# The last quarter of a down projection: six of its eight tiles as Strassen block products

## The chip, the cores and the metric

The kernel runs on one core of a Trainium2 chip, as one launch. The time is device microseconds (us) of that core, from runs of the whole kernel. Smaller is better. The core's engines work beside each other, each through its own instruction stream in order, and wait for one another on semaphores: PE (TensorE, matrix products), DVE (VectorE), ACT (ScalarE), POOL (GpSimd) and SP (which here only issues DMA).

## The reference

Two blocks of a network on 512 positions of 1024 channels, in float32. The change lies in the last step of the second block, a feed-forward layer, and touches the final norm behind it:

```python
h = rms_norm(x, norm2_g[l])
u = causal_dwconv(jnp.einsum('bsd,df->bsf', h, w_up[l]), ffn_conv_w[l])
gate, up = jnp.split(u, 2, axis=-1)
x = x + jnp.einsum('bsf,fd->bsd', jax.nn.gelu(gate) * up, w_down[l])
```

`w_up` is 1024 x 6144 and `w_down` 3072 x 1024. After it the result is normed once more (`final_g`).

## The kernel before, in words

**Layout.** Channels lie on the 128 partitions, positions along the row: `x1[:, j, :]` is tile j (0 to 7) of the result's 1024 channels, 128 x 512. A product in float32 is made of three products of rounded operands (`mm3`, lines 1160 to 1164): high part by high part, low by high, high by low. So each operand needs a high part and a low part. For weights, ACT copies the raw block to the high part (`log_hi`, line 2016) and POOL subtracts it from the raw block for the low part (`log_lo`, line 1128). They go into a ring of 48 blocks of 128 columns, in one fixed order of "steps" (`ffn_steps`, line 307). A step may overwrite blocks only when PE has read what stood there: that is its due tile (`ffn_due`, line 595). ACT's loop `split_weights` (line 2018) takes the steps strictly in order.

**Quarters.** The 3072 inner channels are worked through in four quarters of six tiles. Per quarter PE makes 12 "up" tiles (24 products of 512 columns each), and DVE and ACT turn them into six gated tiles `ff_pre`, split as `ff_hi` and `ff_lo`. One up pair runs ahead, in the next quarter's name.

**Down projection of quarters 0 to 2.** Tiles of the result go in pairs p (2p and 2p+1). Split each way in two (three of six inner tiles, 256 of 512 positions), a pair is a 2 x 2 block product. It is made of seven products n = 1 to 7 (the Winograd form of Strassen's) instead of eight. A product is nine matmuls of 256 columns (`part`, line 1888). Products 1, 6, 7, 4 add up in one PSUM bank, 5 and 3 in bank 6, 2 in bank 7. After each product DVE adds the bank as it then stands to `x1` (`add_part`, line 3297, the add on line 3305). A product that goes on in a bank or opens it anew waits for the last add from it (`open_tile`). The operands of products 4 to 7 are sums: of the weights (`weight_sum`, line 3264, DVE, written to `w_sum` or in place in `raw`; ACT waits for them in `ffn_high`), and of the gated tiles (`t_f32`, split as `t_hi` on line 2441 by ACT and `t_lo` on line 3261 by DVE).

**Down projection of the last quarter.** It is made plainly. `last_down` (line 1912) makes tiles 0 and 1 together, then 2 to 6, each 18 matmuls of 512 columns, then tile 7 in two halves of 256 positions, so that the first half's norm can begin early. Its weights are six steps of 8 blocks, read from three chunks. DVE adds each tile to `x1` (line 2891). ACT then squares it (line 2464, into `sq_acc3` for the first, `sq_last` in four slots after) and multiplies it with the final gain (line 2465, `x_gain`). DVE adds the squares up (`add_square`, line 2904). PE turns `x_gain` to rows (`token_tile`) between and after the halves of tile 7, sums the squares over the partitions, and ACT and DVE scale and write out.

**The order of ACT's end.** All remaining weight splits, then the table for the square root is loaded (line 2459), then the squares and gains in the order of the tiles (lines 2456 to 2465).

Of the kernel before, what the change touches and what calls it, by code (L numbers as in the profile page):

```python
# [289 lines left out]
def part_count(q, p, n):  # L290

    return q * len(PRODUCTS) + PRODUCTS.index((p, n)) + 1


def ffn_chunks():

    out = [("up", 0, 0)]
    for q in range(SEVEN):
        out += [("up", q, i) for i in range(1, FQ)] + [("up", q + 1, 0)]
        out += [("pair", q, p) for p in range(FPAIRS)]  # L300
    return out + [("up", SEVEN, i) for i in range(1, FQ)] + [("down", SEVEN, m) for m in range(KD * FQ * B // CH)]

# [4 lines left out]
def ffn_steps():  # L307

    at, steps = 0, []

    def add(key, chunk, off, width, reader):
        nonlocal at
        n = width // B
        if at % GRAN + n > GRAN:
            at += GRAN - at % GRAN
        steps.append((key, chunk, off, width, at % GRAN, reader))
        at += n

    done = set()
    for c, (kind, q, i) in enumerate(FFN_CHUNKS):  # L320
        if kind == "up":
            for half, name in enumerate(("ff_g", "ff_u")):
                add(("up", q, i, half), c, half * CH // 2, CH // 2, (name, q, i))
        elif kind == "down":
            for half in range(2):
                last = ((2 * i + half + 1) * CH // 2 - 1) // (FQ * B)
                add(("down", i, half), c, half * CH // 2, CH // 2, ("ff_o", q, last))
        elif i == 0:
            for p, n in PRODUCTS:
                add(("form", q, p, n), c + p, RAW_OF.get(n), FORM, ("part", q, p, n))  # L330
    return steps
# [39 lines left out]
def make_plan():  # L371
# [175 lines left out]
    for q in range(SEVEN):  # L547
        for i in range(1, FQ):
            up_tiles(q, i)
        up_tiles(q + 1, 0)  # L550
        for pair, n in PRODUCTS:
            p.add("part", q, pair, n, by=("part_done", part_count(q, pair, n)),
                  bank={2: 7, 5: 6, 3: 6}.get(n, 4 + pair % 2))
    for i in range(1, FQ):
        up_tiles(SEVEN, i)
    for j in range(KD):
        p.add("ff_o", SEVEN, j, by=("resid_done", RES_LAST + j + 1), bank=(6, 7, 4, 0, 1, 2, 3, 4)[j])
    return p
# [51 lines left out]
def build(nc, stream, cols_d, x_d, ctx_d, router_d, wab_d, rope_t_d, dftc_d, ident_d, iota_d, c_rows_d, xt_d, out):  # L610
    with ExitStack() as ctx:
# [119 lines left out]
        sq_acc2 = at("sq_acc2", R + 56, [P, T])  # L731
        sq_acc3 = at("sq_acc3", R + 88, [P, T])

# [222 lines left out]
        def _(sp):  # L956
            sp.dma_start(cols[:], cols_d).then_inc(cols_in, 16)

            def load(n, slot):
                c = CHUNKS[n][1] - FFN_FIRST if CHUNKS[n][0] else -1  # L960
                w = slice(0, 4 * FORM if c >= 0 and FFN_CHUNKS[c][0] == "pair" else CH)
                sp.dma_start(raw[:, slot, w], stream[n, :, w]).then_inc(raw_full[slot], 16)
# [169 lines left out]
        def _(pe):  # L1132
# [774 lines left out]
            def down_block(j, k):  # L1907

                b = j * FQ + k
                return block_of(step_weights("down", b // 16, b % 16 // 8), b % 8)  # L1910

            def last_down(last_half):

                q = SEVEN
                o2 = open_tile("ff_o", q, 0), open_tile("ff_o", q, 1)
                for k in range(FQ):
                    pe.wait_ge(lo_done, SPLITS["ff", q, k] + 1)
                    for i in range(2):
                        last = mm3(o2[i], down_block(i, k), ffx(k, slice(0, T)), k == 0, k == FQ - 1)
                        if k == FQ - 1:  # L1920
                            done(last)
                for j in range(2, KD - 1):
                    o = open_tile("ff_o", q, j)
# [27 lines left out]
            def token_tile(n):  # L1951

                t, half = Y_TILES[n]
                o = psum[:, Y_BANKS[n], :]
                pe.wait_ge(x_gain_done, KD - 1 if half else 4)
                if half:
                    pe.wait_ge(resid_done, RES_LAST + KD + t // 2)
                if n == 2:
                    pe.wait_ge(resid_done, RES_LAST + 5)
                if n >= 6 or n == 4:  # L1960

                    pe.wait_ge(resid_done, RES_LAST + KD + (n >= 6))
                if n in (5, 7):
# [37 lines left out]
        def _(act):  # L2001
# [428 lines left out]
            def operands(q, i):  # L2430

                g = q * FQ + i
                act.wait_ge(pre_done, pf + g + 1)
                if i == 0 and q >= 1:
                    full(act, "part", q - 1, *PRODUCTS[-1])
                if q < SEVEN and i < FK:
                    A(t_f32[:, i, 2, :], ff_pre[:, g % 2, FH:T], ACT.Copy).then_inc(v_kept, 1)
                hi(ff_hi[:, i, :], ff_pre[:, g % 2, :])
                if q < SEVEN and i >= FK:
                    act.wait_ge(t_sum, 4 * FK * q + FK + 3 * (i - FK) + 3)  # L2440
                    A(t_hi[:, i - FK, :, :], t_f32[:, i - FK, :, :], ACT.Copy).then_inc(t_hi_done, 1)

            for q in range(QUARTERS):
# [5 lines left out]
                if q < SEVEN:  # L2449
# [5 lines left out]
                    operands(q + 1, 0)  # L2455
            for j in range(KD):
                split_weights(TILE["ff_o", SEVEN, j])
            assert nsplit[0] == NSTEPS
            nc.scalar.preload_act_table(ACT.Sqrt)
            for j in range(KD - 1):  # L2460
                act.wait_ge(resid_done, RES_LAST + j + 1)
                if j > 4:
                    act.wait_ge(sq_added, added[0] + j - 4)
                A(sq_acc3[:] if j == 0 else sq_last[:, (j - 1) % 4, :], x1[:, j, :], ACT.Square).then_inc(sq_done, 1)
                A(x_gain[:, j, :], x1[:, j, :], ACT.Copy, scale=col("final_g_2", j)).then_inc(x_gain_done, 1)

# [31 lines left out]
        def _(dve):  # L2498
# [720 lines left out]
            def gated(q, i):  # L3219
# [88 lines left out]
            for q in range(QUARTERS):  # L3308
                for i in range(0 if q == 0 else 1, FQ):
# [3 lines left out]
                    gated(q, i)  # L3313
                    if q < SEVEN and i >= FK:
# [5 lines left out]
                    if q < SEVEN:  # L3320
                        if i == 1:
                            first_term(q, 0)
                        if 1 <= i < FK:
                            first_term(q, i)
                        if i > FK:
                            low_terms(q, i - FK - 1)
                        if i == FK - 1:
                            weight_sums(q, 0, SUM_OF)
                        if i == FK:
                            weight_sums(q, 1, (5, 7, 6))  # L3330
# [9 lines left out]
                for i, (p, m) in enumerate(PRODUCTS):  # L3340
# [204 lines left out]
```

## Time and profile before

| | us |
|---|---|
| median of 3 runs | 1278.86 (1278.36 to 1280.0) |
| profiled execution, its own time | 1279.63 |
| span in its trace | 1277.7 |
| PE busy in the span | 1262.7 |
| DVE, ACT, POOL busy | 748.0, 510.1, 509.2 |
| mean granted clock of PE | 0.995 of full |

The profile's page lists busy times of the engines and the chain of work that ended last. The trace behind it gives each instruction with its start in the span. A line such as "x3" merges instructions in a row; the duration is then that of the stretch. A matmul's duration is modelled and overlaps the next one's, so PE's pace is read from the distance of the starts. An entry in brackets is how long the engine stood idle before, and who released it.

### The profile page before, as it was taken

The page shows a single profiled execution, that of the slowest core. Times are in us where ns is not written, and L with a number is a line of the kernel's source. Part 1 is how long each engine was busy: PE and PEld are TensorE (multiplying, and loading weights), DVE is VectorE, ACT ScalarE, POOL GpSimd, SP SyncE. Part 2 cuts the span into 40 slices and gives each one's busy share as a digit, 9 for nine tenths or more (in the row PEclk, how much of TensorE's full clock was granted, in tenths as well). Part 3 has the DMA queues.
Part 4 walks back from the last instruction along what each step waited for, and adds up shares of the span by engine and source line. Part 5 has one row for each costly group of instructions (what it writes and reads, how often), then busy time and mean ns, then how long its engine had stood idle before and what let it go on. Part 6 is the DMA issues. An engine that isn't in the chain of part 4 may idle for free.

```text
span 1277.7 us, 16609 instructions
## 1 busy us (share of the span) xinstructions
PE 1262.7 (99%) x6439; PEld 942.4 (74%) x6439; DVE 748.0 (59%) x1335; ACT 510.1 (40%) x765; POOL 509.2 (40%) x284
## 2 busy tenths in 40 slices
PE   8999999999999999999999999999999999999998
PEld 6789888766687544444366788888889889889887
DVE  2487986877864434323368458322786586576453
ACT  4353324476333211111156742433454345344343
POOL 3154457277330000000142252544458458548530
PEclk9999999999999899999999999999999999999999
DMA  9534585001257999999942131322123323313301
GB/s 373 239 125 189 199 335 190 33 34 57 76 203 291 357 425 427 426 426 426 427 163 97 67 103 63 132 99 99 52 67 122 107 72 120 131 47 122 122 1 66
DMA packets 34350, 227.13 MB, mean 178 GB/s; under 512 B 3936, under 2 KB 4576, under 8 KB 9440
## 3 DMA queue, kind: packets, MB, share of 16 engines
q1 hardware_dynamic: 31536, 216.63, 44.0%
q10 hardware_dynamic: 1584, 5.24, 1.1%
q0 software_dynamic: 1152, 4.19, 0.9%
q8 instruction: 52, 0.85, 0.3%
q14 instruction: 26, 0.21, 0.1%
HBM read 221.86 MB, written 4.19 MB: 177 GB/s over the span
## 4 chain that ended last, share of the span: by engine, by line
PE 90%; DVE 6%; ACT 2%; DMA 1%; issue 1%; POOL 0%; SPq 0%; DVEq 0%; ACTq 0%
PE psum L1162 22%; PE psum L1164 22%; PE psum L1163 22%; PE psum L1718 13%; PE psum L1493 2%; PE psum L1458 1%; DVE x L2893 1%; DMA x<-in_x 1%; PE psum L1803 1%; DVE psum L3203 1%; PE psum L1700 1%; PE psum L1675 1%; PE psum L1703 1%; PE psum L1181 0%; PE psum L1658 0%
## 5 line engine op out<-in xcount | busy, mean ns | idle before, releaser
L1128 POOL TENSOR_TENSOR log_lo<-raw,log_hi 128x1024 fp32r<-128x1024 f32 (+1 forms) x102 | 181.8, 1808 | 131.1 <-ACT log_hi L2016 130.9
L1077 POOL TENSOR_TENSOR w_lo<-raw,w_hi 128x1024 fp32r<-128x1024 f32 x43 | 106.0, 2465 | 310.8 <-ACT w_hi L2037 305.4
L1162 PE MATMUL psum<-b_hi,log_hi 128*128 128x512 f32 x384 | 149.7, 390 | 0.0
L1164 PE MATMUL psum<-b_hi,log_lo 128*128 128x512 f32 x384 | 149.4, 389 | 0.0
L1163 PE MATMUL psum<-b_lo,log_hi 128*128 128x512 f32 x384 | 149.4, 389 | 0.0
L1081 POOL TENSOR_TENSOR w_lo<-raw,w_hi 128x1024 fp32r<-128x1024 f32 x43 | 112.0, 2605 | 0.0
L2037 ACT ACTIVATE w_hi<-raw 128x2048 fp32r<-128x2048 f32 (+1 forms) x44 | 83.3, 1892 | 43.8 <-PE psum L1164 23.5
L1718 PE MATMUL psum<-ex_ring,xe 128*64 128x512 f32 x424 | 93.2, 594 | 0.0
L1162 PE MATMUL psum<-b_hi,w_hi 128*128 128x512 f32 x224 | 88.5, 395 | 0.2 <-DVE b_lo L2938 0.2
L1164 PE MATMUL psum<-b_hi,w_lo 128*128 128x512 f32 x224 | 87.2, 389 | 0.0
L1163 PE MATMUL psum<-b_lo,w_hi 128*128 128x512 f32 x224 | 87.2, 389 | 0.0
L1164 PEld LDWEIGHTS psum<-b_hi,log_lo 128*128 128x128 f32 x384 | 72.1, 188 | 15.1
L1163 PEld LDWEIGHTS psum<-b_lo,log_hi 128*128 128x128 f32 x384 | 72.1, 188 | 14.9
L1162 PEld LDWEIGHTS psum<-b_hi,log_hi 128*128 128x128 f32 x384 | 72.1, 188 | 14.7
L2016 ACT ACTIVATE log_hi<-raw 128x1024 fp32r<-128x1024 f32 (+1 forms) x102 | 77.9, 795 | 8.5 <-PE psum L1164 8.5
L1162 PE MATMUL psum<-h_hi,w_hi 128*128 128x512 f32 x200 | 79.8, 399 | 1.3 <-POOL w_lo L1056 1.0
L1091 POOL DMA_INDIRECT xg<-xt,ids x8 | 7.7, 959 | 181.6 <-PE psum L1703 127.0
L1164 PE MATMUL psum<-h_hi,w_lo 128*128 128x512 f32 x200 | 78.0, 390 | 0.0
L1163 PE MATMUL psum<-h_lo,w_hi 128*128 128x512 f32 x200 | 77.9, 390 | 0.0
L1718 PEld LDWEIGHTS psum<-ex_ring,xe 128*64 128x64 f32 x424 | 29.8, 137 | 58.2 <-issue 58.0
L2893 DVE SCALAR_TENSOR_TENSOR x<-psum,mod,x 128x512 f32<-128x512 f32 x72 | 50.5, 744 | 24.9 <-PE psum L1164 20.2
L3203 DVE TENSOR_TENSOR psum<-psum,rstd_s 128x512 f32<-128x512 f32 x48 | 33.3, 695 | 45.3 <-PE psum L1164 45.2
(513 smaller groups left out, 2968.7 us busy)
## 6 DMA issues: line engine op xcount, KB each, us to landing
raw<-in_stream SPq DMA_DIRECT2D x88, 1024.0 KB, 4.9
ex_ring<-in_stream SPq DMA_DIRECT2D x77, 1024.0 KB, 16.1
ex_more<-in_stream SPq DMA_DIRECT2D x18, 1024.0 KB, 17.2
raw<-in_stream SPq DMA_DIRECT2D x12, 768.0 KB, 4.2
mod_in<-in_stream SPq DMA_DIRECT2D x8, 1024.0 KB, 19.8
x<-in_x SPq DMA_DIRECT2D x4, 512.0 KB, 6.7
x<-in_x ACTq DMA_DIRECT2D x1, 2048.0 KB, 8.5
xt<-h2t ACTq DMA_DIRECT2D x8, 256.0 KB, 3.3
```

The lines of the kernel that those rows point to most:

```text
L1077: nc.gpsimd.tensor_tensor(w_lo[:, slot, w], raw[:, raw_slot, w], w_hi[:, slot, w].bitcast(F32), ALU.subtract)
L1081: nc.gpsimd.tensor_tensor(w_lo[:, slot, w], raw[:, raw_slot, w], w_hi[:, slot, w].bitcast(F32), ALU.subtract).then_inc(w_lo_done, 1)
L1128: nc.gpsimd.tensor_tensor(lo_, src, hi_.bitcast(F32), ALU.subtract).then_inc(w_lo_done, 1)
L1162: mm(o, w[0], x[0], start=start, stop=False, skip_group_check=goes_on)
L1163: mm(o, w[0], x[1], start=False, stop=False, skip_group_check=goes_on)
L1164: return mm(o, w[1], x[0], start=False, stop=stop, skip_group_check=goes_on)
L1493: last = mm(psum[s * VD:s * VD + VD, 6 + h % 2, :], v[:, k + s, h * VD:h * VD + VD], probs[k + s][:], start=k == 0, stop=k == KT - 2)
L1718: last = mm(o[e * CAP:(e + 1) * CAP, :], x_of(k, e), w[:, (2 * (k - k0) + e) * T:(2 * (k - k0) + e + 1) * T], start=k == 0, stop=k == ks - 1)
L2016: A(dst, src, ACT.Copy).then_inc(w_hi_done, 1)
L2037: A(w_hi[:, c % NHL, w], raw[:, n % NRAW, w], ACT.Copy).then_inc(w_hi_done, 1)
L2893: ins = V.scalar_tensor_tensor(out=x1[:, j, :], in0=o, scalar=scale, in1=x1[:, j, :], op0=ALU.mult, op1=ALU.add)
L3203: V.tensor_tensor(o, o, rstd, ALU.mult).then_inc(ffz_done, 1)
```

## The change

The last quarter's down projection is made in the manner of the others for tiles 0 to 5 (three pairs), tile 6 stays plain and comes fourth, and tile 7 stays in halves at the end. The last quarter's gated tiles and weights get the sums that this needs. The squares go in the order 6, 0, 1, 2, 3, 4, 5. The weights come as three pair chunks and one plain chunk with tiles 6 and 7 (40 chunks instead of 39, 1536 columns wide each). The steps are 21 of 3 blocks and two of 6. Some buffers move (`sq_acc3`, `sq_last`) because the operand sums now fill their old place. The core of the diff:

```diff
+def last_order():
+    out = [(p, 1) for p in range(LAST_PAIRS)] + [LAST_TILE]
+    out += [(0, 2), (1, 2), (0, 5), (0, 6), (0, 3), (0, 7), (1, 5), (0, 4)]
+    out += [(1, 6), (1, 3), (1, 7), (2, 5), (1, 4)]
+    return out + [(2, n) for n in (6, 3, 7, 2, 4)]
+LAST_Y, LAST_X = (4, 5, 0), (1, 2, 7)
+LAST_SUMS = {(0, 3): 5, (0, 7): 7, (1, 5): 6, (0, 4): 3}
+LAST_SQUARES = {(1, 6): (1,), (1, 7): (2,), (1, 4): (3,), (2, 7): (4,), (2, 4): (5, 6)}
+LAST_TILES = (KD - 2, *range(KD - 2))
+def part_bank(q, p, n):
+    if n in (5, 3):
+        return 6
+    if n == 2:
+        return 7 if q < SEVEN else LAST_X[p]
+    return 4 + p % 2 if q < SEVEN else LAST_Y[p]
+def part_of_tile(j):
+    return max(part_count(SEVEN, j // 2, n) for n in ((5, 7, 4) if j % 2 else (1, 2, 6, 3)))
...
@@ PE, last_down
+                for p, n in LAST_ORDER:
+                    if (p, n) != LAST_TILE:
+                        part(q, p, n)
+                        continue
+                    o = open_tile("ff_o", q, KD - 2)
                     for k in range(FQ):
-                        last = mm3(o, down_block(j, k), ffx(k, slice(0, T)), k == 0, k == FQ - 1)
+                        pe.wait_ge(lo_done, SPLITS["ff", q, k] + 1)
+                        last = mm3(o, down_block(KD - 2, k), ffx(k, slice(0, T)), k == 0, k == FQ - 1)
                     done(last)
                 open_tile("ff_o", q, KD - 1)
                 for s in range(2):
+                    if s == 1:
+                        pe.wait_ge(part_done, part_count(q, 1, 4))
...
@@ PE, token_tile
-                pe.wait_ge(x_gain_done, KD - 1 if half else 4)
+                pe.wait_ge(x_gain_done, KD - 1 if half else 5)
+                if n == 0:
+                    pe.wait_ge(part_done, part_count(SEVEN, *LAST_ORDER[-1]))
...
@@ ACT
-                if q < SEVEN and i < FK:
+                if i < FK:
                     A(t_f32[:, i, 2, :], ff_pre[:, g % 2, FH:T], ACT.Copy).then_inc(v_kept, 1)
...
-            for j in range(KD):
-                split_weights(TILE["ff_o", SEVEN, j])
+            for p, n in LAST_ORDER:
+                split_weights(TILE["ff_o", SEVEN, KD - 2] if (p, n) == LAST_TILE else TILE["part", SEVEN, p, n])
             assert nsplit[0] == NSTEPS
             nc.scalar.preload_act_table(ACT.Sqrt)
-            for j in range(KD - 1):
-                act.wait_ge(resid_done, RES_LAST + j + 1)
-                if j > 4:
-                    act.wait_ge(sq_added, added[0] + j - 4)
-                A(sq_acc3[:] if j == 0 else sq_last[:, (j - 1) % 4, :], x1[:, j, :], ACT.Square).then_inc(sq_done, 1)
+            for i, j in enumerate(LAST_TILES):
+                if i == 0:
+                    act.wait_ge(resid_done, RES_LAST + 1)
+                else:
+                    act.wait_ge(part_done, part_of_tile(j))
+                if i > 4:
+                    act.wait_ge(sq_added, added[0] + i - 4)
+                A(sq_acc3[:] if i == 0 else sq_last[:, (i - 1) % 4, :], x1[:, j, :], ACT.Square).then_inc(sq_done, 1)
                 A(x_gain[:, j, :], x1[:, j, :], ACT.Copy, scale=col("final_g_2", j)).then_inc(x_gain_done, 1)
...
@@ DVE (the guards "if q < SEVEN" around terms, first_term, low_terms and weight_sums go)
-            dve.wait_ge(part_done, SEVEN * len(PRODUCTS))
-            for j in range(KD - 1):
-                residual(j, ("ff_o", SEVEN, j), RES_LAST)
-                add_square(3, j, sq_acc3, sq_last, 4)
+            for p, m in LAST_ORDER:
+                if (p, m) == LAST_TILE:
+                    residual(KD - 2, ("ff_o", SEVEN, KD - 2), RES_LAST)
+                    continue
+                add_part(SEVEN, p, m)
+                if (p, m) == (1, 2):
+                    weight_sum(SEVEN, 1, 3)
+                if (p, m) in LAST_SUMS:
+                    weight_sum(SEVEN, 2, LAST_SUMS[p, m])
+                for i in LAST_SQUARES.get((p, m), ()):
+                    add_square(3, i, sq_acc3, sq_last, 4)
```

`add_square(3, i, ...)` waits until ACT has made i + 1 of the last norm's squares, adds square i, and waits for its own end. The tile 6 has the name `LAST_TILE`.

## Rows read from the trace of the kernel before

**Rows 1.** The page: PE's busy time, and the chain that ended last.

```profile
PE 1262.7 (99%) x6439; PEld 942.4 (74%) x6439; DVE 748.0 (59%) x1335; ACT 510.1 (40%) x765; POOL 509.2 (40%) x284
...
PE 90%; DVE 6%; ACT 2%; DMA 1%; issue 1%; POOL 0%; SPq 0%; DVEq 0%; ACTq 0%
```

**Rows 2.** Timeline, PE, last down projection (start, duration, instruction): first, last, first half-width matmul.

```profile
1234.23 0.39 PE L1162 MATMUL psum<-ff_hi,log_hi 128*128 128x512 f32 x1
...
1262.56 0.39 PE L1164 MATMUL psum<-ff_hi,log_lo 128*128 128x512 f32 x1
1262.79 0.28 PE L1162 MATMUL psum<-ff_hi,log_hi 128*128 128x256 f32 x1
```

**Rows 3.** Busy time by stretch (PE, PEld, DVE, ACT, POOL, clock, DMA): tiles 0 to 6.

```profile
1234.20:1262.80 28.60, 28.60 (x128) 23.66 (x127) 11.72 (x17) 11.44 (x17) 2.40 (x1) 1.00 0.00 1
```

**Rows 4.** Timeline, PE, third quarter's 28 products: first, at its short stall, next stage.

```profile
1149.30 0.28 PE L1162 MATMUL psum<-ff_hi,log_hi 128*128 128x256 f32 x1
...
1154.58 0.28 PE L1164 MATMUL psum<-ff_hi,log_lo 128*128 128x256 f32 x1
1154.78 0.39 PE L1162 MATMUL psum<-ff_hi,log_hi 128*128 128x256 f32 x1
...
1179.80 0.40 PE L1162 MATMUL psum<-b_hi,log_hi 128*128 128x512 f32 x1
```

**Rows 5.** Timeline, DVE, third quarter: low parts of the operands, weight sums, adds.

```profile
1143.39 1.29 DVE L2513 TENSOR_TENSOR ff_lo<-ff_pre,ff_hi 128x512 fp32r<-128x512 f32 x2
1144.59 3.18 DVE L3261 TENSOR_TENSOR t_lo<-t_f,t_hi 128x1024 fp32r<-128x1024 f32 x2
...
1150.59 0.55 DVE L3287 TENSOR_TENSOR w_sum<-raw,w_sum 128x384 f32<-128x384 f32 x1
...
1153.97 0.76 DVE L3305 TENSOR_TENSOR x<-psum,x 128x256 f32<-128x256 f32 x2
...
1166.36 1.04 DVE L3281 TENSOR_TENSOR raw<-raw 128x384 f32<-128x384 f32 x1
```

**Rows 6.** Timeline, POOL: low part of a weight step of 384 and of 1024 columns.

```profile
1151.83 1.02 POOL L1128 TENSOR_TENSOR log_lo<-w_sum,log_hi 128x384 fp32r<-128x384 f32 x1 [3.18 <-ACT log_hi L2016]
...
1239.84 2.40 POOL L1128 TENSOR_TENSOR log_lo<-raw,log_hi 128x1024 fp32r<-128x1024 f32 x1 [6.01 <-ACT log_hi L2016]
```

**Rows 7.** Timeline, ACT, third quarter: three weight splits in a row.

```profile
1162.39 1.33 ACT L2016 ACTIVATE log_hi<-raw 128x384 fp32r<-128x384 f32 x3
```

**Rows 8.** Timeline, ACT, last quarter: last split, table load, first squares and gains, last gain.

```profile
1238.72 1.04 ACT L2016 ACTIVATE log_hi<-raw 128x1024 fp32r<-128x1024 f32 x1
1239.78 1.28 ACT L2459 ACT_TABLE_LOAD   x1
1242.71 0.63 ACT L2464 ACTIVATE sq_acc<-x 128x512 f32<-128x512 f32 x1 [1.64 <-DVE x L2891]
1243.24 0.71 ACT L2465 ACTIVATE x_gain<-x,cols 128x512 f32<-128x512 f32 x1
1243.86 0.61 ACT L2464 ACTIVATE sq_last<-x 128x512 f32<-128x512 f32 x1
...
1264.32 0.71 ACT L2465 ACTIVATE x_gain<-x,cols 128x512 f32<-128x512 f32 x1
```

**Rows 9.** Timeline, DVE, last quarter: the last sum of squares of the plain tiles.

```profile
1264.45 0.69 DVE L2904 TENSOR_TENSOR sq_acc<-sq_acc,sq_last 128x512 f32<-128x512 f32 x1 [0.70 <-ACT sq_last L2464]
```

**Rows 10.** Busy time by stretch, where PE's granted clock (third from last) fell and rose.

```profile
402.00:403.00 1.00, 1.00 (x8) 1.00 (x8) 0.73 (x4) 0.94 (x1) 0.00 (x0) 0.56 0.96 393
...
405.00:406.00 1.00, 1.00 (x6) 0.70 (x6) 0.00 (x0) 0.30 (x1) 0.00 (x0) 0.73 1.03 434
...
1272.00:1273.00 1.00, 0.94 (x9) 0.75 (x7) 0.88 (x4) 0.39 (x1) 0.00 (x0) 1.00 1.01 414
...
1276.00:1277.00 1.00, 0.00 (x0) 0.00 (x0) 0.00 (x0) 0.00 (x0) 0.00 (x0) 0.50 0.78 320
```

More of the change, by code:

```diff
@@ L277 @@
 PRODUCTS = product_order()
+LAST_PAIRS, LAST_TILE = 3, (KD - 2, 0)
+def last_order():
[3 more added lines that the diff above has]
+    return out + [(2, n) for n in (6, 3, 7, 2, 4)]
+LAST_ORDER = last_order()
+LAST_PRODUCTS = [step for step in LAST_ORDER if step != LAST_TILE]
+LAST_Y, LAST_X = (4, 5, 0), (1, 2, 7)
+LAST_SUMS = {(0, 3): 5, (0, 7): 7, (1, 5): 6, (0, 4): 3}
+LAST_SQUARES = {(1, 6): (1,), (1, 7): (2,), (1, 4): (3,), (2, 7): (4,), (2, 4): (5, 6)}
+LAST_TILES = (KD - 2, *range(KD - 2))
 OUT_OF = {1: (0, 0), 2: (0, 0), 5: (1, 1), 6: (0, 1), 7: (1, 1), 3: (0, 1), 4: (1, 0)}
@@ L300, in ffn_chunks @@
         out += [("pair", q, p) for p in range(FPAIRS)]
-    return out + [("up", SEVEN, i) for i in range(1, FQ)] + [("down", SEVEN, m) for m in range(KD * FQ * B // CH)]
+    out += [("up", SEVEN, i) for i in range(1, FQ)] + [("pair", SEVEN, p) for p in range(LAST_PAIRS)]
+    return out + [("down", SEVEN, 0)]
 FFN_CHUNKS = ffn_chunks()
@@ L324, in ffn_steps @@
         elif kind == "down":
-            for half in range(2):
-                last = ((2 * i + half + 1) * CH // 2 - 1) // (FQ * B)
-                add(("down", i, half), c, half * CH // 2, CH // 2, ("ff_o", q, last))
+            add(("down", KD - 1), c, FQ * B, FQ * B, ("ff_o", q, KD - 1))
         elif i == 0:
-            for p, n in PRODUCTS:
-                add(("form", q, p, n), c + p, RAW_OF.get(n), FORM, ("part", q, p, n))
+            for p, n in PRODUCTS if q < SEVEN else LAST_ORDER:
+                if (p, n) == LAST_TILE:
+                    add(("down", KD - 2), c + LAST_PAIRS, 0, FQ * B, ("ff_o", q, KD - 2))
+                else:
+                    add(("form", q, p, n), c + p, RAW_OF.get(n), FORM, ("part", q, p, n))
     return steps
@@ L552, in make_plan @@
             p.add("part", q, pair, n, by=("part_done", part_count(q, pair, n)),
-                  bank={2: 7, 5: 6, 3: 6}.get(n, 4 + pair % 2))
+                  bank=part_bank(q, pair, n))
     for i in range(1, FQ):
         up_tiles(SEVEN, i)
-    for j in range(KD):
-        p.add("ff_o", SEVEN, j, by=("resid_done", RES_LAST + j + 1), bank=(6, 7, 4, 0, 1, 2, 3, 4)[j])
+    for pair, n in LAST_ORDER:
+        if (pair, n) == LAST_TILE:
+            p.add("ff_o", SEVEN, KD - 2, by=("resid_done", RES_LAST + 1), bank=7)
+        else:
+            p.add("part", SEVEN, pair, n, by=("part_done", part_count(SEVEN, pair, n)), bank=part_bank(SEVEN, pair, n))
+    p.add("ff_o", SEVEN, KD - 1, by=("resid_done", RES_LAST + 2), bank=LAST_BANKS[0])
     return p
@@ L731, in build @@
         sq_acc2 = at("sq_acc2", R + 56, [P, T])
-        sq_acc3 = at("sq_acc3", R + 88, [P, T])
+        sq_acc3 = at("sq_acc3", R + 8, [P, T])
         router_g = at("router_g", R + 88, [P, KD, 32])
@@ L960, in load @@
                 c = CHUNKS[n][1] - FFN_FIRST if CHUNKS[n][0] else -1
-                w = slice(0, 4 * FORM if c >= 0 and FFN_CHUNKS[c][0] == "pair" else CH)
+                w = slice(0, 4 * FORM if c >= 0 and FFN_CHUNKS[c][0] != "up" else CH)
                 sp.dma_start(raw[:, slot, w], stream[n, :, w]).then_inc(raw_full[slot], 16)
@@ L1907, in down_block @@
             def down_block(j, k):
-                b = j * FQ + k
-                return block_of(step_weights("down", b // 16, b % 16 // 8), b % 8)
+                return block_of(step_weights("down", j), k)
             def last_down(last_half):
                 q = SEVEN
[L1915 to L1923, printed above, removed]
+                for p, n in LAST_ORDER:
[3 more added lines that the diff above has]
+                    o = open_tile("ff_o", q, KD - 2)
                     for k in range(FQ):
-                        last = mm3(o, down_block(j, k), ffx(k, slice(0, T)), k == 0, k == FQ - 1)
+                        pe.wait_ge(lo_done, SPLITS["ff", q, k] + 1)
+                        last = mm3(o, down_block(KD - 2, k), ffx(k, slice(0, T)), k == 0, k == FQ - 1)
                     done(last)
@@ L2435, in operands @@
                     full(act, "part", q - 1, *PRODUCTS[-1])
-                if q < SEVEN and i < FK:
+                if i < FK:
                     A(t_f32[:, i, 2, :], ff_pre[:, g % 2, FH:T], ACT.Copy).then_inc(v_kept, 1)
                 hi(ff_hi[:, i, :], ff_pre[:, g % 2, :])
-                if q < SEVEN and i >= FK:
+                if i >= FK:
                     act.wait_ge(t_sum, 4 * FK * q + FK + 3 * (i - FK) + 3)
@@ L2455, in _ @@
                     operands(q + 1, 0)
-            for j in range(KD):
-                split_weights(TILE["ff_o", SEVEN, j])
+            for p, n in LAST_ORDER:
+                split_weights(TILE["ff_o", SEVEN, KD - 2] if (p, n) == LAST_TILE else TILE["part", SEVEN, p, n])
             assert nsplit[0] == NSTEPS
             nc.scalar.preload_act_table(ACT.Sqrt)
-            for j in range(KD - 1):
-                act.wait_ge(resid_done, RES_LAST + j + 1)
-                if j > 4:
-                    act.wait_ge(sq_added, added[0] + j - 4)
-                A(sq_acc3[:] if j == 0 else sq_last[:, (j - 1) % 4, :], x1[:, j, :], ACT.Square).then_inc(sq_done, 1)
+            for i, j in enumerate(LAST_TILES):
+                if i == 0:
+                    act.wait_ge(resid_done, RES_LAST + 1)
+                else:
+                    act.wait_ge(part_done, part_of_tile(j))
+                if i > 4:
+                    act.wait_ge(sq_added, added[0] + i - 4)
+                A(sq_acc3[:] if i == 0 else sq_last[:, (i - 1) % 4, :], x1[:, j, :], ACT.Square).then_inc(sq_done, 1)
                 A(x_gain[:, j, :], x1[:, j, :], ACT.Copy, scale=col("final_g_2", j)).then_inc(x_gain_done, 1)
@@ L3226, in gated @@
                     dve.wait_ge(lo_done, SPLITS["ff", before[0], before[1]] + 1)
-                    if before[0] < SEVEN and before[1] < FK:
+                    if before[1] < FK:
                         dve.wait_ge(v_kept, before[0] * FK + before[1] + 1)
@@ L3313, in _ @@
                     gated(q, i)
-                    if q < SEVEN and i >= FK:
+                    if i >= FK:
                         terms(q, i - FK)
@@ L3319, in _ @@
                         low_of(q, i)
[L3320 to L3330, printed above, removed]
+                    if i == 1:
+                        first_term(q, 0)
+                    if 1 <= i < FK:
+                        first_term(q, i)
+                    if i > FK:
+                        low_terms(q, i - FK - 1)
+                    if i == FK - 1:
+                        weight_sums(q, 0, SUM_OF)
+                    if i == FK:
+                        weight_sums(q, 1, (5, 7, 6))
+                low_terms(q, FK - 1)
                 if q == SEVEN:
                     continue
-                low_terms(q, FK - 1)
                 factor(0, q + 1, 0)
```

16 lines of the change are left out of this document (7 added, 9 removed).

## The prediction

> **What bounds the kernel now.** I read the page first. PE is busy 99% of the span and makes 90% of the chain that ended last; DVE has 6%, ACT 2% [rows 1]. Time goes away only where PE gets less to do or waits less. Then the stage that is changed, in the timeline of PE: its first matmul starts at 1234.23, tile 7 starts at 1262.79 [rows 2]. That is 28.56 us for seven tiles of 18 matmuls, so 0.2267 us a matmul and 4.08 us a tile, without a gap, at full clock, while DVE and ACT are busy 12 us each and POOL 2.4 [rows 3]. PE alone sets this stage, and the others have room on average. What they do in which order is another matter, and on that this forecast rests.
>
> **The gain.** The third quarter shows how fast such products run: from 1149.30 to the start of its last matmul before the stall at 1154.58 there are 44 steps, 0.120 us each [rows 4]. A product of nine is 1.08 us. The change takes away 6 x 4.08 = 24.48 us and brings 21 x 1.08 = 22.68 us. It saves 1.80 us, 0.14% of the time. It is less than an eighth of 24.48 (3.06), because two matmuls of 256 columns take 0.240 us where one of 512 takes 0.2267. Tiles 6 and 7 cost what they cost. A difference under about 0.2% (2.6 us) can't be told from none here, so even the whole gain would be "no change".
>
> **The new stage, step by step.** I count from T = 0, where PE ends the last up tile (1234.23 before).
>
> *The operands' low parts.* PE makes (0,1), (1,1), (2,1), tile 6, (0,2), (1,2) by 9.48; these need only `ff_hi`, `ff_lo`. Then (0,5) needs the last `t_lo`. In the third quarter the matching T is 1149.30 less one up pair (48 x 0.2267 = 10.88), 1138.42. `ff_lo` ended at 1144.68, 6.3 behind it, in time for tile 6's last inner tile at 6.64; the two `t_lo` ended at 1147.77, 9.35 behind it [rows 5]. So (0,5) starts at 9.5, just in time. In the third quarter a whole up pair covered this; the cover is gone, and 0 to 0.5 us could show.
>
> *DVE's backlog.* Only now, at 9.3, does DVE reach the adds. Each takes 0.34 us in a row (0.76 for two [rows 5]). Three adds, tile 6 (0.6), two adds, the weight sum 3 of pair 1 (0.5 alone), the add of (0,5): it is done at 12.5. (0,3) goes on in bank 6 and waits for that add; it would have started at 11.6. PE stands 0.9 us. The third quarter shows the same kind of wait, 0.08 us, at the same product [rows 4].
>
> *The sums of pair 2.* They are made after the adds of (0,3), (0,7), (1,5), (0,4). Such a sum takes 0.55 us while POOL is idle, and up to 1.04 while POOL works [rows 5]; POOL takes 1.0 for a step of 384 columns [rows 6]. The add of (0,4) ends at 17.9, the last sum, n = 3, at 19.0 (at 18.0 if it never has to stand behind POOL).
>
> *Where it jams.* ACT splits weights strictly in order, and (2,3) needs that last sum. So at 19.1 ACT still has five splits before it: (2,3), (2,7), (2,2), (2,4), 0.42 each [rows 7], and tile 7's 768 columns, 0.84 between 0.51 and 1.04 by its width [rows 7, 8]. Then it loads the table, 1.28, and only then come square 6, gain 6 and square 0: 0.53 + 0.62 + 0.62 [rows 8]. Sum: 1.68 + 0.84 + 1.28 + 1.77 = 5.6. Square 0 ends at 24.7. Meanwhile DVE has added (1,6) and stands in `add_square(1)`, the sum of square 0, from about 19.3. Behind that wait in DVE's queue stand the adds of (1,3) and (1,7). PE makes (1,7) until 20.5 and then wants bank 6 for (2,5), which is free only after the add of (1,3). POOL has work until then too: seven low parts, the last (tile 7, between 1.0 and 2.4 [rows 6], 1.8) from 23.8 to 25.6, and the sum of squares reads two operands from SBUF like the weight sums, so it stands behind it: 25.6 to 26.3 (0.69 alone [rows 9]), the add of (1,3) to 26.7, and (2,5) starts at 26.8. Without any wait it would start at 14 x 1.08 + 4.08 = 19.2. The delay is 7.6 us.
>
> *Behind it.* Squares 1 to 3 find ACT ahead, at 1.15 a tile against PE's 7 products. PE goes on without waits to 26.8 + 7 x 1.08 = 34.4. Before it was 28.56, so tile 7 starts 5.8 us later (7.6 less 1.8).
>
> *The tail.* Tile 5 is complete with the add of (2,4), at about 0.6 after tile 7's start; before, tile 6 was complete at about 0.95. Last gain before: 1264.32 + 0.71, 2.2 after it [rows 8]; now 2.0 to 2.1. Nothing before the end of tile 7's first half (2.2) needs more, so the 14.9 us from 1262.79 to the span's end stay, to within 0.2.
>
> *Up tiles of the last quarter.* They get DVE's sums and ACT's copies as in the third, where the up tiles ran without a gap on PE; I cost them at 0. Their cover is 5.44 us of PE per up tile. DMA: four chunks of 768 KB for three of 1024, each landing long before; 0.
>
> **The clock.** PE now stands about 6 us. In the trace, PE's work ends in the stretch 1272 to 1273, and by 1276 to 1277 the granted clock is 0.50, the lower level, 1.2 GHz for 2.4; earlier in the span it fell in the stretch 402 to 403 and rose in 405 to 406, about 3.4 us, after PE had done only thin work [rows 10]. So I expect a fall during the wait, and PE at half pace for some us after it. Bounds: 0, if it rises as PE resumes or never falls, and 3.4 us, if it stays low for twice that 3.4 us stretch after the wait. I take 1.4, nearer to one such stretch, partly in the wait. The Trainium skill (TensorE: Matmul & The Clock Gate, section "HAM oscillation — how this bites in real kernels") says that a wait of PE between bursts puts its clock back to half. That speaks against this change; the tail's rows agree as to the fall, and no row shows a burst after so long a wait.
>
> A second page bears on the term for the table load. The row shows 1.28 us, starting 0.02 after the split before it [rows 8]. The Trainium skill (ScalarE: Activation LUTs, section "What ACT_TABLE_LOAD costs") puts a further drain of about 1.38 us on every switch. By it the square would come 1.4 later and (2,5) some 0.5 later, since POOL's last low part covers the rest. The trace shows no such drain here.
>
> **Sum.** +5.8 + 1.4 = +7.2 us. The profiled execution took 1279.63 (span 1277.7, 1.9 around it), 0.77 above the median; the same 7.2 on it is 1286.8, on the median 1286.1.
>
> **Bounds.** Downward: sums and squares never behind POOL, DVE without backlog. Then the last sum ends at 17.0 to 17.1, square 0 at 22.7, the add of (1,3) at 23.9, and (2,5) is 4.7 late: +2.9, 1281.8. Upward: 5.8, clock 3.4: +9.2, 1288.1, and up to 0.9 more for a low part or `t_lo` behind POOL: 1289.
>
> **Rivals.**
> 1. *The wait on squares doesn't bite; the whole gain comes* (not slower). It would need ACT to reach square 0 before DVE asks, at 19.3 instead of 24.7. For it: ACT is busy only 40% of the time in this stage [rows 3], and if its splits were done with product (0,3), as their due tiles allow, it would be on the squares by 17. The point that decides is whether split (2,3) must wait for DVE's sum behind (0,4): by `ffn_high` it does. Then 1.8 less the 0.9 of the backlog or none of it: -0.9 to -1.8, 1277.1 to 1278.0. Chance 0.12, for a misreading of one of five links (sum, split order, square, add, bank).
> 2. *The jam is there, but the clock doesn't fall or costs nothing*: +2.9 to +5.8, 1281.8 to 1284.7. Against it: the rows on the clock. 0.3.
> 3. *The jam and a long slow stretch*: clock 1.7 to 3.4 and the full collision with POOL, 1286.4 to 1289. 0.25.
> 4. *A new wait ahead of the jam*: `t_lo` late behind POOL or DVE late in the up tiles, so that PE stalls several us at (0,5). The third quarter has 9.35 for a need at 9.48, so 0.5 more at most; it comes on top of the others and doesn't decide.
>
> The forecast (jam, and 0.5 to 1.7 for the clock) has 0.33. Together the jam has 0.88. "Slower by over 0.2%" starts at 1281.4, below every case of the jam but a shortened one (0.02): slower 0.86, same 0.12, faster 0.02, since even the full 1.8 is not 0.2%. The range 1281.7 to 1289 leaves out rival 1 and some of the ends.
>
> **What would show each step.** The products at 0.120 us a matmul; (0,3) 0.5 to 1 us late; ACT idle until a sum on line 3287's counterpart, then splits, table load, square and gain of tile 6, square 0 without a gap; DVE idle 5 to 6 us ahead of a sum of squares, released by ACT's square; PE idle about 6 us ahead of the first matmul of (2,5), released by a DVE add; a granted clock of 0.50 in some stretch about there. If PE has no gap over 1 us in this stage, my reading of the order is wrong. If the gap is there and the clock is full, only that term is.

## The result, and the profile after

| | before | changed |
|---|---|---|
| median, 6 runs each | 1279.32 us (1278.36 to 1280.67) | 1285.3 us (1284.18 to 1287.48) |
| profiled execution, span | 1277.7 us | 1283.5 us |
| last up tile's end to tile 7's start | 28.56 us | 35.54 us |
| tile 7's start to the span's end | 14.9 us | 14.9 us |

The ratio is 1.005, 95% interval 1.0038 to 1.0061: the kernel is slower, by 6.0 us between the medians and 6.4 by the ratio. The page's line of busy times and the line of the chain that ended last, to set against [rows 1]:

```profile
PE 1259.1 (98%) x6520; PEld 943.0 (73%) x6520; DVE 772.5 (60%) x1377; ACT 518.5 (40%) x788; POOL 519.7 (40%) x301
...
PE 87%; DVE 8%; ACT 2%; DMA 1%; issue 1%; POOL 0%; SPq 0%; DVEq 0%; ACTq 0%; POOLq 0%
```

PE is busy 3.6 us less and the span is 5.8 us longer, and 3% of the chain went from PE mostly to DVE. Where that happened is seen in the timeline of PE in the new stage, against [rows 2, 4] (start, duration, instruction; in brackets the idle time and who ended it). Here (p, n) is product n of pair p:

```profile
1233.05 0.28 PE L1201 MATMUL psum<-ff_hi,log_hi 128*128 128x256 f32 x1
...
1242.54 0.28 PE L1201 MATMUL psum<-t_hi,log_hi 128*128 128x256 f32 x1
...
1244.58 0.28 PE L1203 MATMUL psum<-t_hi,log_lo 128*128 128x256 f32 x1
1245.50 0.39 PE L1201 MATMUL psum<-ff_hi,log_hi 128*128 128x256 f32 x1 [0.64 <-DVE x L3345]
...
1253.06 0.28 PE L1203 MATMUL psum<-t_hi,log_lo 128*128 128x256 f32 x1
1259.16 0.58 PE L1201 MATMUL psum<-t_hi,log_hi 128*128 128x256 f32 x1 [5.82 <-DVE x L3345]
1259.54 0.41 PE L1202 MATMUL psum<-t_lo,log_hi 128*128 128x256 f32 x1
...
1263.16 0.32 PE L1201 MATMUL psum<-t_hi,log_hi 128*128 128x256 f32 x1
1263.32 0.28 PE L1202 MATMUL psum<-t_lo,log_hi 128*128 128x256 f32 x1
...
1268.59 0.28 PE L1201 MATMUL psum<-ff_hi,log_hi 128*128 128x256 f32 x1
```

T = 0 is 1233.05. PE waits twice, both times for a DVE add: 0.80 us ahead of (0,3), and 5.98 ahead of (2,5), by the starts less one step of 0.12. The brackets count from the modelled end of the matmul before and give 0.64 and 5.82. Behind the second wait, 18 matmuls take 4.00 us, 0.22 each instead of 0.120; that is 1.84 us more. Then the pace is full again up to tile 7 at 1268.59. The account of the stage: 26.76 of products (21 x 1.08 + 4.08), 0.80, 5.98, 1.84, and 0.16 of small pieces make 35.54.

Who was late is read from ACT, DVE and POOL. ACT's timeline, against [rows 8]:

```profile
1251.71 0.53 ACT L2053 ACTIVATE log_hi<-w_sum 128x384 fp32r<-128x384 f32 x1 [0.77 <-DVE w_sum L3327]
1252.14 2.07 ACT L2053 ACTIVATE log_hi<-raw 128x384 fp32r<-128x384 f32 x4
1254.23 1.28 ACT L2496 ACT_TABLE_LOAD   x1
1255.52 0.63 ACT L2504 ACTIVATE sq_acc<-x 128x512 f32<-128x512 f32 x1
1256.06 0.71 ACT L2505 ACTIVATE x_gain<-x,cols 128x512 f32<-128x512 f32 x1
1256.67 0.61 ACT L2504 ACTIVATE sq_last<-x 128x512 f32<-128x512 f32 x1
```

DVE's, against [rows 5, 9]:

```profile
1239.21 3.17 DVE L3301 TENSOR_TENSOR t_lo<-t_f,t_hi 128x1024 fp32r<-128x1024 f32 x2
...
1250.59 1.03 DVE L3327 TENSOR_TENSOR w_sum<-raw,w_sum 128x384 f32<-128x384 f32 x1
1251.54 0.41 DVE L3345 TENSOR_TENSOR x<-psum,x 128x256 f32<-128x256 f32 x1
1257.32 1.32 DVE L2944 TENSOR_TENSOR sq_acc<-sq_acc,sq_last 128x512 f32<-128x512 f32 x1 [5.37 <-ACT sq_last L2504]
1258.68 0.76 DVE L3345 TENSOR_TENSOR x<-psum,x 128x256 f32<-128x256 f32 x2
```

And POOL's:

```profile
1239.67 1.62 POOL L1167 TENSOR_TENSOR log_lo<-w_sum,log_hi 128x384 fp32r<-128x384 f32 x1 [5.93 <-ACT log_hi L2053]
...
1253.43 4.66 POOL L1167 TENSOR_TENSOR log_lo<-raw,log_hi 128x384 fp32r<-128x384 f32 x4
```

The last of the four in the merged lines of ACT ("x4") and POOL is tile 7's, 768 columns wide. DVE's last weight sum ends at T = 18.6. ACT then does five splits, the table load, square 6, gain 6 and square 0 without a gap, and square 0 ends at 24.2. DVE stands in front of it for 5.37 us, with the add of (1,3) behind it in its queue. The sum of squares then takes 1.32 us instead of 0.69 [rows 9]: it runs while POOL's last low part does, and ends 0.55 behind it (1258.09). Two adds follow, and the first frees bank 6 for (2,5).

The clock, by stretches of 1 us (third number from the end), against [rows 10]:

```profile
1253.00:1254.00 1.00, 0.34 (x3) 0.13 (x2) 0.00 (x0) 1.00 (x3) 1.00 (x2) 1.00 0.00 0
...
1256.00:1257.00 1.00, 0.00 (x0) 0.00 (x0) 0.00 (x0) 1.00 (x3) 1.00 (x2) 0.70 0.00 0
1257.00:1258.00 1.00, 0.00 (x0) 0.00 (x0) 0.68 (x1) 1.00 (x3) 1.00 (x1) 0.50 0.00 0
...
1263.00:1264.00 1.00, 1.00 (x9) 1.00 (x9) 0.60 (x2) 0.14 (x1) 0.00 (x0) 0.89 0.00 0
```

PE's last matmul starts at 1253.06; the clock falls in the stretch 1256 to 1257 to its lower level, 1.2 GHz, and rises in 1263 to 1264, 4 us after PE resumed. By the shares in these stretches it is low from about 1256.4 to 1263.2, 2.8 us of it while PE still waits and 4.0 behind.

The span grew by 5.8 and the stage by 6.98, because this execution of the changed kernel reached the stage 1.18 us earlier than the one of before, in code that the change doesn't touch. The executions differ there: in the one of before the granted clock is at its lower level from 402 to 405 and 415 to 422 [rows 10 show the first], in this one nowhere from 380 to 440, but PE waits 2.2 us for a gather. What makes up the 1.18 us was not followed further. So small differences are read from the stage, not from whole runs: over the study, runs of the kernel before lie between 1276.8 and 1282.7.

### The profile page after: what moved, and what is told of

Read it like the earlier page. It is cut to its first block, busy times and chain, and to the rows that moved or that the text cites. A ratio compares the mean times of both kernels' runs of the same rounds, so it can differ in the third digit from the quotient of the medians.

```text
span 1283.5 us, 16918 instructions
## 1 busy us (share of the span) xinstructions
PE 1259.1 (98%) x6520; PEld 943.0 (73%) x6520; DVE 772.5 (60%) x1377; ACT 518.5 (40%) x788; POOL 519.7 (40%) x301
## 4 chain that ended last, share of the span: by engine, by line
PE 87%; DVE 8%; ACT 2%; DMA 1%; issue 1%; POOL 0%; SPq 0%; DVEq 0%; ACTq 0%; POOLq 0%
PE psum L1201 22%; PE psum L1203 21%; PE psum L1202 21%; PE psum L1757 13%; PE psum L1532 2%; PE psum L1497 1%; DVE x L2933 1%; DMA xg<-xt,ids 1%; DMA x<-in_x 1%; DVE psum L3243 1%; PE psum L1842 1%; PE psum L1714 1%; PE psum L1739 1%; DVE t_lo L3301 0%; PE psum L1742 0%
## 5 line engine op out<-in xcount | busy, mean ns | idle before, releaser
L1167 POOL TENSOR_TENSOR log_lo<-raw,log_hi 128x384 fp32r<-128x384 f32 (+1 forms) x110 | 183.6, 1693 | 120.5 <-ACT log_hi L2053 120.5
L2053 ACT ACTIVATE log_hi<-raw 128x384 fp32r<-128x384 f32 (+1 forms) x110 | 78.8, 750 | 8.2 <-PE psum L1203 8.2
L1167 POOL TENSOR_TENSOR log_lo<-w_sum,log_hi 128x384 fp32r<-128x384 f32 x45 | 52.4, 1175 | 50.2 <-ACT log_hi L2053 50.2
## 6 DMA issues: line engine op xcount, KB each, us to landing
ex_more<-in_stream SPq DMA_DIRECT2D x18, 1024.0 KB, 18.1
```

What stands on the lines that cost most here:

```text
L1167: nc.gpsimd.tensor_tensor(lo_, src, hi_.bitcast(F32), ALU.subtract).then_inc(w_lo_done, 1)
L2053: A(dst, src, ACT.Copy).then_inc(w_hi_done, 1)
```

## The experiments

Two theories of the slowdown stood against each other. **Order**: the late square 0 holds DVE, DVE holds bank 6, the bank holds PE, and the clock adds its part. **Weights or width**: POOL's low parts of the weights come late for pair 2, or narrow products are dearer than their pace. "Stage" below is from the last up tile's end to tile 7's start in the run's own trace: 28.56 before, 35.54 changed.

**Squares asked for later.**

```diff
-LAST_SQUARES = {(1, 6): (1,), (1, 7): (2,), (1, 4): (3,), (2, 7): (4,), (2, 4): (5, 6)}
+LAST_SQUARES = {(2, 3): (1,), (2, 7): (2,), (2, 2): (3,), (2, 4): (4, 5, 6)}
```

> Edit: the changed kernel, with DVE's sums of squares asked for later: square 1 after (2,3), 2 after (2,7), 3 after (2,2), 4 to 6 after (2,4). Nothing else moves. Theory (ACT's order makes square 0 late, DVE waits for it ahead of the add of (1,3), PE waits for that add): the gap of 5.8 us ahead of (2,5) and the slow clock behind it (about 1.7 us) go; the wait of 0.6 us ahead of (0,3) stays. Tile 7 starts about 27.5 us after the last up tile, against 35.5 in the changed kernel and 28.6 in the one before; about 1278.3 us, ratio to before 0.9985 to 1.000. Rival (weights: the low parts from POOL are what comes late for the products of pair 2): the gap stays at 3 us or more, now released by POOL, and the time stays above 1282. Rival (the narrow products themselves are dearer than their pace): no gap, but over 1281.

Measured: 1279.37 us, ratio 0.9998 (0.9987 to 1.0009). The timeline of PE has one wait left:

```profile
1236.91 0.28 PE L1201 MATMUL psum<-ff_hi,log_hi 128*128 128x256 f32 x1
...
1249.36 0.39 PE L1201 MATMUL psum<-ff_hi,log_hi 128*128 128x256 f32 x1 [0.64 <-DVE x L3345]
...
1264.61 0.28 PE L1201 MATMUL psum<-ff_hi,log_hi 128*128 128x256 f32 x1
```

The stage is 27.70 us, for 27.5 expected. The gap of 5.98 and the 1.84 of slow clock are both gone with one line of when DVE asks, though the weights come when they came: POOL's low parts of pair 2 start at T = 18.1 and the last ends at 25.2, against 18.1 and 25.0 in the changed kernel. The rivals of late weights and of dear products fall.

**Table load earlier.** `preload_act_table` moved ahead of ACT's last loop of splits.

```diff
+            nc.scalar.preload_act_table(ACT.Sqrt)
             for p, n in LAST_ORDER:
                 split_weights(...)
             assert nsplit[0] == NSTEPS
-            nc.scalar.preload_act_table(ACT.Sqrt)
```

> Edit: the changed kernel, with the table of the square root loaded before ACT's last loop of weight splits (ACT is idle for 5.6 us there) instead of behind it. Theory: the chain from DVE's last weight sum to square 0 loses the 1.28 us of the load and nothing else; square 0 ends about 22.9 us after the last up tile instead of 24.2, and since DVE then asks for its port between two low parts of POOL, the gap ahead of (2,5) shrinks by 1.2 to 2.0 us to 3.8 to 4.6 us. The clock may still fall. Time 1282.5 to 1284.3. If the load had a hidden drain behind it, the gap would shrink by more than 2.5. Rival (POOL's low parts release PE): no change of the gap.

Measured: 1284.62 us, ratio 1.0045 (1.003 to 1.0061), stage 32.59. PE, DVE and ACT:

```profile
1256.83 0.58 PE L1201 MATMUL psum<-t_hi,log_hi 128*128 128x256 f32 x1 [4.07 <-DVE x L3345]
```

```profile
1239.43 2.35 DVE L3301 TENSOR_TENSOR t_lo<-t_f,t_hi 128x1024 fp32r<-128x1024 f32 x2
...
1255.32 1.00 DVE L2944 TENSOR_TENSOR sq_acc<-sq_acc,sq_last 128x512 f32<-128x512 f32 x1 [3.94 <-ACT sq_last L2504]
```

```profile
1239.42 1.28 ACT L2493 ACT_TABLE_LOAD   x1
1240.72 0.53 ACT L2053 ACTIVATE log_hi<-w_sum 128x384 fp32r<-128x384 f32 x1
```

The gap is 4.07 by the bracket, against 5.82, and in the range of 3.8 to 4.6. From the end of the last weight sum to the end of square 0 it is 4.24 us instead of 5.66, 1.42 less for a load of 1.28, so the load was a link of the chain at about its own length; the other 0.3 is the sum of squares, 1.00 for 1.32. The stage fell by 2.95, more than the gap did: the wait ahead of (0,3) went too, which was not expected. The two low parts of the operands take 2.35 us here against 3.17 in the changed kernel and 3.18 in the third quarter [rows 5], because ACT's next split, and so POOL's low part, comes after them and not between. The slow stretch was shorter too in this execution, and cost about 0.4 less: the clock rose in the stretch 1259 to 1260. The median lies 0.3 above the expected 1282.5 to 1284.3; the stage alone, 4.03 longer than before, would put it at 1282.9.

**PE kept busy in the gap.** Its products are thrown away.

```diff
+                    if (p, n) == (2, 5):
+                        pe.wait_ge(accu_done, QUARTERS * FQ)
+                        for _ in range(24):
+                            mm(psum[:, 3, :], ff_hi[:, 0, 0:B], ff_hi[:, 0, :], start=True, stop=True)
```

> Edit: the changed kernel, with 24 matmuls of 512 columns (5.4 us, results overwritten later in bank 3) on PE ahead of (2,5), where it stands idle. Theory of two terms (jam 5.8 us, and a slow clock of 4 us behind it that costs 1.7): PE's filling ends before the add of (1,3), so the jam stays as it is to within 0.1 us, but the granted clock stays at 1.00 and the products of (2,5) and (1,4) run at 0.120 us a matmul instead of 0.213. About 1.7 us less than the changed kernel: 1283.2 to 1284.0. Rival (the slow stretch is not set by the idle time): the clock still falls and the time is as in the changed kernel, 1285.3, or higher by what the filling overlaps.

Measured: 1284.15 us, ratio 1.0048 (1.003 to 1.0067), stage 33.90, 1.64 less than in the changed kernel. PE:

```profile
1251.76 5.63 PE L1957 MATMUL psum<-ff_hi 128*128 128x512 f32 x24
1257.86 0.39 PE L1201 MATMUL psum<-t_hi,log_hi 128*128 128x256 f32 x1 [0.47 <-DVE x L3349]
```

```profile
1257.00:1258.00 1.00, 0.53 (x3) 0.15 (x2) 0.96 (x3) 0.79 (x3) 0.00 (x0) 1.00 0.00 0
1258.00:1259.00 1.00, 1.00 (x9) 1.00 (x10) 0.73 (x2) 1.00 (x2) 0.00 (x0) 1.00 0.08 16
```

(2,5) starts at T = 26.2 as in the changed kernel (26.1), and the clock stays full. So the slow stretch is what the idle PE costs on top, and the jam is the rest. The median lies 0.15 above the range; the stage, which the spread ahead of it doesn't touch, gives 1.64 for the 1.7 expected.

**Squares 1 and 2 together after (1,7).**

```diff
-LAST_SQUARES = {(1, 6): (1,), (1, 7): (2,), ...
+LAST_SQUARES = {(1, 7): (1, 2), ...
```

> Edit: the changed kernel, with the sum of square 1 asked for after the add of (1,7), together with square 2, instead of after (1,6). Theory: the adds of (1,3) and (1,7) are made before DVE stands still, so (2,5), (1,4) and (2,6) run without a wait, and the jam comes at (2,3), which goes on in bank 6 and needs the add of (2,5) behind the two sums of squares: these end at about 26.5 us after the last up tile, the add at 26.9, against 23.3 for a (2,3) without a wait. Gap about 3.6 us instead of 5.8, ahead of (2,3); with the clock still falling up to 1.7, otherwise 0 behind it. Time 1281.3 to 1283.5. Rival (PE waits for something of pair 2 as such): the gap stays ahead of (2,5).

Measured: 1284.02 us, ratio 1.0037 (1.0023 to 1.0051), stage 33.12. PE, then the clock:

```profile
1258.11 0.28 PE L1203 MATMUL psum<-t_hi,log_lo 128*128 128x256 f32 x1
1261.77 0.39 PE L1201 MATMUL psum<-ff_hi,log_hi 128*128 128x256 f32 x1 [3.38 <-DVE x L3345]
```

```profile
1262.00:1263.00 1.00, 1.00 (x9) 0.90 (x8) 0.96 (x3) 0.93 (x2) 0.00 (x0) 1.00 0.00 0
1263.00:1264.00 1.00, 0.95 (x6) 0.85 (x6) 0.52 (x2) 0.32 (x1) 0.00 (x0) 0.70 0.00 0
...
1266.00:1267.00 1.00, 1.00 (x7) 1.00 (x7) 0.31 (x1) 0.00 (x0) 0.00 (x0) 0.59 0.00 0
```

The gap moved to (2,3), as foretold, with 3.4 us for 3.6. It is not pair 2 as such that waits, it is whatever needs DVE's next add. The clock fell here (0.70 in the stretch 1263 to 1264, so at about 1263.4) though PE had resumed 1.6 us before, and it stayed low for 3.4 us, which cost about 1.5. The median lies 0.5 above the expected 1281.3 to 1283.5; the stage alone, 4.56 longer than before, would put it at 1283.4.

**Both mended.** The edits of the first two together.

> Edit: both of the first two experiments together: sums of squares asked for later, and the table load ahead of ACT's last loop of splits. The trace of the table alone showed the wait ahead of (0,3) gone too, since ACT's split of (1,6), and with it POOL's low part, then comes after DVE's second low part of the operands instead of between. Theory: no wait of PE over 0.2 us between the last up tile and tile 7, which starts 26.8 us after the last up tile (21 x 1.08 + 4.08 = 26.76) against 27.7 with late squares alone and 28.56 in the kernel before. That is the whole gain of 1.8 us: ratio 0.9975 to 0.9995. Rival (the wait ahead of (0,3) is of another cause, and was gone by chance): it is back at 0.6 us and the stage takes 27.4 to 27.7.

Measured: 1278.56 us, ratio 0.9994 (0.9982 to 1.0005). PE has no wait that the profile reports:

```profile
1232.80 0.28 PE L1201 MATMUL psum<-ff_hi,log_hi 128*128 128x256 f32 x1
...
1259.69 0.28 PE L1201 MATMUL psum<-ff_hi,log_hi 128*128 128x256 f32 x1
```

The stage is 26.89 us, 1.67 less than before. On whole runs that can't be told from no change. It is nearly the 1.80 that the products have to give, read from one execution of each kernel, and the spread of the rest covers it.

**ACT's order instead of DVE's.** DVE's requests as in the change; ACT makes squares and gains of tiles 6 and 0 after the split of (1,4), with the table loaded early.

```diff
+            nc.scalar.preload_act_table(ACT.Sqrt)
             for p, n in LAST_ORDER:
                 split_weights(...)
+                if (p, n) == (2, 1):
+                    square_gain(0, LAST_TILES[0])
+                    square_gain(1, LAST_TILES[1])
             assert nsplit[0] == NSTEPS
-            nc.scalar.preload_act_table(ACT.Sqrt)
```

> Edit: the changed kernel with DVE's requests where they were, but ACT's order changed: table load before the last loop of splits, and squares and gains of tiles 6 and 0 directly behind the split of (1,4), ahead of the splits of (2,6) to tile 7. Theory (the jam lies in ACT's order alone): square 0 ends about 19.4 us after the last up tile, when DVE asks for it at 19.0, so no gap ahead of (2,5); square 1 comes behind the remaining splits at about 22, where DVE waits 1 to 2 us without holding PE up. Tile 7 starts 26.8 to 27.6 after the last up tile. Rival (weights bind): the splits of pair 2 now come 2.3 us later, so if the low parts of pair 2 were what PE waited for, the gap is 5.8 or longer, released by POOL.

Measured: 1279.8 us, ratio 1.0001 (0.999 to 1.0011), stage 27.36. ACT and DVE:

```profile
1249.11 0.61 ACT L2501 ACTIVATE sq_last<-x 128x512 f32<-128x512 f32 x1
```

```profile
1250.71 0.68 DVE L2951 TENSOR_TENSOR sq_acc<-sq_acc,sq_last 128x512 f32<-128x512 f32 x1
...
1253.69 1.08 DVE L2951 TENSOR_TENSOR sq_acc<-sq_acc,sq_last 128x512 f32<-128x512 f32 x1 [1.05 <-ACT sq_last L2501]
```

Square 0 is made 1.0 us before DVE asks, and the sum of squares follows the add of (1,6) with no wait. The splits of pair 2 did not come 2.3 us later, as expected: that of (2,6) came 0.2 later than in the change, the rest 0.7 earlier, because the wait ahead of (0,3) is gone here too. But POOL's low parts of pair 2, which the rival blames, start at T = 18.1 in both and the last ends later, at 26.2 against 25.0, and still the gap is gone. The early table load can't be what ended it, since alone it left 4.07. DVE's wait for square 1, 1.05 us, was expected to hold nothing up; with the adds behind it late, (2,3) and (2,7) start late, and the stage is 0.47 longer than in the run before. The same jam is undone from the other side, so its place is the order on ACT against the order on DVE.

**(1,6) ahead of (0,3).** With the squares asked for later.

```diff
-    out += [..., (0, 5), (0, 6), (0, 3), (0, 7), (1, 5), (0, 4)]
-    out += [(1, 6), (1, 3), (1, 7), (2, 5), (1, 4)]
+    out += [..., (0, 5), (0, 6), (1, 6), (0, 3), (0, 7), (1, 5), (0, 4)]
+    out += [(1, 3), (1, 7), (2, 5), (1, 4)]
```

> Edit: late squares (first experiment), and product (1,6) moved ahead of (0,3), the table load back where the change has it. Theory of the wait ahead of (0,3) (DVE's backlog makes the add of (0,5) 0.6 to 0.9 us late): one more product, 1.08 us, between (0,5) and (0,3) covers it; the wait goes or is under 0.1 us, and tile 7 starts 26.8 to 26.9 us after the last up tile instead of 27.7. Rival (PE waits there for something else, such as the low parts of the weights): the wait stays at 0.64.

Measured: 1278.53 us, ratio 0.9994 (0.9982 to 1.0006), stage 27.42, not the 26.8 to 26.9 expected. The wait ahead of (0,3) is gone, which is what the run was for. Another showed up at the last product:

```profile
1260.12 0.38 PE L1201 MATMUL psum<-t_hi,log_hi 128*128 128x256 f32 x1 [0.40 <-DVE x L3345]
```

```profile
1258.17 1.44 DVE L2944 TENSOR_TENSOR sq_acc<-sq_acc,sq_last 128x512 f32<-128x512 f32 x1
1259.64 0.42 DVE L3345 TENSOR_TENSOR x<-psum,x 128x256 f32<-128x256 f32 x1
```

```profile
1254.28 4.78 POOL L1167 TENSOR_TENSOR log_lo<-raw,log_hi 128x384 fp32r<-128x384 f32 x4
```

Square 0 is ready at 1258.14, only 0.1 us after the add of (2,3). But its sum runs beside POOL's last low part, which ends at 1259.06, and takes 1.44 us instead of 0.69; it ends 0.55 behind POOL, as in the changed kernel. The next add, for which (2,4) waits, comes behind it. With late squares alone the add of (2,3) starts at T = 24.7 and POOL ends at 25.2; here it starts at 23.7 and POOL still ends at 25.2, so the sum meets more of POOL's work.

## Why the prediction was right

It gave 1286.1 us and a range of 1281.7 to 1289; measured were 1285.3. Every link of the chain it named is in the traces, and the experiments bear out the order as the cause. The closeness of the total owes something to luck: the wait was sized 0.7 us too long and the clock 0.4 too short, and the two offset each other in part. By its steps:

- **The gain.** 0.120 us a matmul and 1.80 us in all: the run with both mends shows 1.67 in the stage.
- **`t_lo` in time.** Right: the last `t_lo` ends at T = 9.33, for 9.35 foretold, and (0,5) starts without a wait, at 1242.54 (T = 9.49).
- **DVE's backlog ahead of (0,3).** 0.9 foretold, 0.80 by the starts. That it is DVE's add is confirmed by one more product in between, which removes it. What the step took as given and could be had otherwise: 0.8 us of that backlog is the `t_lo` beside one of POOL's low parts, 3.17 us in the five traces with the table load late and 2.35 in the three with it early.
- **The last sum.** Foretold to end at T = 19.0, it ended at 18.6.
- **The jam.** The order sum, splits, load, square 6, gain 6, square 0 came to 5.6 us, as foretold (24.2 less 18.6). The wait ahead of (2,5) was 5.98; foretold were 6.7 (the 7.6 less the 0.9 that PE had stood already). Of the 0.7 too many, 0.4 comes from the earlier last weight sum. The collision of the sum of squares with POOL's last low part was there, but cost 0.6, not the 0.9 from 24.7 to 25.6. The start of (2,5), 26.1 for 26.8, is the term that was sized too large.
- **The clock.** 1.4 foretold, 1.84 measured, 1.64 by the run that keeps PE busy. It was sized too small: the forecast took nearly one stretch of 3.4 us, partly in the wait, where the clock was low for 6.8 us, 2.8 of them in the wait and 4.0 behind it. The Trainium skill (TensorE: Matmul & The Clock Gate, section "HAM oscillation — how this bites in real kernels") says that a wait between bursts of matmuls puts PE's clock back to half. The trace agrees: 0.50 in the stretch 1257 to 1258.
- **The table load.** 1.28 us with 0.01 us to the next instruction behind it; moved to a place where ACT goes on at once, the next split starts 0.02 after it. The Trainium skill (ScalarE: Activation LUTs, section "What ACT_TABLE_LOAD costs") names a further drain of about 1.38 us for each switch of the set. It doesn't show in either place; the measurement decides.
- **The tail.** 14.9 us on both sides, as foretold.
- **The sum.** +7.2 foretold, +6.98 in the stage: 0.1 less for the backlog, 0.7 less for the wait, 0.4 more for the clock, 0.16 of small pieces. On the medians it is 6.0 to 6.4: the part of the kernel ahead of the stage varies by more than the rest of the error.

Rival 1 (the squares don't hold PE up) fell with the trace of the change and with the first experiment; its -0.9 to -1.8 is what the stage gains when they really don't (-0.86 with late squares, -1.67 with both mends). Rival 2, an unharmed clock, fell with the clock's rows. Rival 3's clock term came, if only just: 1.84 is outside the 0.5 to 1.7 that the forecast's chance was given for and inside rival 3's 1.7 to 3.4. Its time, 1286.4 or more, did not, because the jam was shorter. Rival 4's new wait ahead of (0,5) did not come.

## What to carry to other kernels

A change that saves work on the bound engine brings nothing if a helper's strict queue then holds that engine up: follow each queue through the stage, and look for an instruction that waits for something which another queue makes only after all its own other work. Here one early request for a square, whose sum nothing used until ACT took its buffer again 16 us later, cost 6 us of waiting and 1.8 us of clock on top. Moving either side of the dependence ended it: one line in DVE's order, or a few in ACT's with the table load moved too. And where the mended kernel gains less than its runs vary, the stage's own length in the trace can tell what the medians can't.

## What the runs showed of the hardware that was not expected

- The clock can fall after PE has resumed: with an idle time of 3.4 us it fell 1.6 us after the first new matmul, and about 1.5 us were lost all the same (squares 1 and 2 together).
- The place of one POOL instruction went with what two DVE instructions with both operands in SBUF took, 2.35 or 3.17 us, in all eight traces with the new stage. In the seven that keep the order of the products, it went with whether PE waited 0.8 us three microseconds later: in four of four with 3.17, in none of three with 2.35.
- The table load took 1.28 us in both places, and the next instruction started 0.01 to 0.02 us behind it.
- The untouched part of the kernel differs by up to 5.3 us between executions in these traces (the last up tile ends at 1231.62 to 1236.91), with a granted clock that falls in some and not in others, between 402 and 436 us. The fall does not explain it alone: the execution that reaches the stage first, at 1231.62, has it.
